# Retention values finished and evicted block by block, and a new order of VectorE's work in the input layer

## The chip, the cores and the metric

The kernel runs on one core of a Trainium2 chip. The time is the device time of one execution in microseconds (us), the median of several runs. The core has five engines that run side by side, each with its own queue of instructions: TensorE (PE in the profile, its weight loads PEld), VectorE (DVE), ScalarE (ACT), GpSimd (POOL) and SyncE (SP), which here only issues the loads from memory (HBM). They wait for one another by semaphores.

## What is computed

Two blocks of a language model in float32, for 512 tokens of width 1024. The change lies in the input layer of the first block:

```
n = _rms_norm(h, attn_norm_w[l])
proj = jnp.einsum('bsd,dc->bsc', n, w_in[l])
(gq, gk, gv, gg, ga, gb, rq, rk, rv, rg) = jnp.split(proj, split_idx, axis=-1)
o_gdn = _gated_deltanet(gq, gk, gv, gg, ga, gb, ...)
o_ret = _retention(rq, rk, rv, rg)
```

`rv` are the values of the retention, four heads of 128 columns. `rq` and `rk` are its queries and keys, which are rotated (`_xpos_rotary`) before use. The gated delta net needs, for each of 4 blocks of 128 tokens and each of 4 heads (16 tiles of 128x128), a matrix M and the inverse of I + M, and a masked product of queries and keys:

```
decay = jnp.exp(jnp.where(causal, diff, -jnp.inf))
m = jnp.where(strict, jnp.einsum('nbhik,nbhjk->nbhij', kb, kc) * decay, 0.0)
t_mat = lax.linalg.triangular_solve(eye + m, jnp.broadcast_to(eye, m.shape), ...)
qk = jnp.einsum('nbhik,nbhjk->nbhij', qc, kc) * decay
```

## The kernel before

**Projections.** Every projection is a matmul of 512 tokens by weights. A *unit* `u` is 128 output columns over the whole contraction of 1024, and is made of two *halves*, 2u and 2u+1, each over 512 of the contraction. float32 is split in a high and a low part, so that each product is three matmuls (lines 1930 to 1932, the helper `three`): a half is 12 matmuls of 128x512, a unit 24. The output lies in one of PSUM's banks 0 to 3, unit u in bank u mod 4; banks 4 to 7 (`MX`) are for the small matmuls of the delta net and the retention. Unit u may start when the bank of unit u-4 has been emptied: TensorE waits for `bank_free`, a counter that rises by one with each eviction.

**Weights.** They arrive by *pair* of units (p = u // 2), 1 MB in two transfers of 512 KB, into a buffer `raw` of two slots. ScalarE rounds a half to its high part (`split_hi(n)`, line 660, output `w_hi`), GpSimd makes the low part (`split_lo(n)`, line 539, output `w_lo`). Both buffers are rings of four halves: `split_hi(n)` waits until half n-4 has been used up (`half_done`, n-3), and until its pair has landed. SyncE issues pair p when the low parts of pair p-2 are made. So pair 10 (units 20 and 21, halves 40 to 43) is issued when `w_lo` of half 35 is there, and pair 11 when that of half 39 is.

**Units 12 to 15** are the retention's values, computed as one *wide* matmul: the 512 tokens are four blocks of 128 rows (one bank each), the 512 value columns are the moving side. Halves 24 to 31 are here the eight 128-rows of the contraction, k = 0 to 7. `wide_half(n)` runs one k over all four blocks, so all four banks are complete only at the end of k = 7. VectorE then empties them with a scale per token, `RCOL` (line 1514, output `ret_v`).

**Units 16 to 23** are the queries and keys of the retention. VectorE empties each by two instructions, `rotate_first` (lines 1299 and 1300: a product with the cosine, output `rq` or `rk`, and a shuffle of partitions, output `scratch`, which frees the bank), and finishes it by `rotate_second` (lines 1306 and 1307).

**The delta net beside them.** ScalarE takes the exponentials of two decay arrays, `T` and `M`, 128x2048 each (lines 832 and 834, semaphore `decay_exp`). VectorE makes M of its one by two products (lines 1471 and 1472, `m_ready`), and masks T (line 1480, by `UPPER`, called `masks` in the profile). T's last column goes to `KDC` (line 1483, output `small`) and T times the query-key product in banks 4 to 7 to `QKT` (line 1485, `qkt_ready`). For the inverses of the 8x8 blocks on M's diagonal, ScalarE cuts four pieces of M (line 839, `blocks_cut`) and writes the identity (line 841), VectorE reduces them (`cut_blocks`, lines 1354 to 1358) and eliminates (`eliminate(k)` for k = 1 to 6, lines 1363, 1366 and 1368). Line 1487 spreads the result over T (`t2_ready`). Between the two halves of unit 21 TensorE transposes T's 16 tiles (`t_transposes`, line 2154), and after unit 21 the levels of the inverse begin.

**What sets the order.** Everything is written out by hand: each engine's program is a loop over u, with `if u == ...` for the work beside the projections. An engine runs its instructions strictly in that order. GpSimd has one wait of its own: it starts the low parts of half 34 only after `m_ready` (before them, in its program, stand halves 32 and 33). In VectorE's program stand at u = 14 the two products of M, at u = 15 the four evictions of the values, and at u = 16 `rotate_first(16)`, the inverses, the mask on T, `KDC`, `QKT`, line 1487, and then `rotate_second(16)`, the rotations of 17, 18 and 19.

Of the kernel before, what the change touches and what calls it, by code (L numbers as in the profile page):

```python
# [9 lines left out]
P = 128  # L10
S = 512
D = 1024
KT = D // P
NB = S // P
H = 4
# [18 lines left out]
ACT = mybir.ActivationFunctionType  # L34
# [34 lines left out]
BK = 8  # L69
# [59 lines left out]
def build(nc, a, const, out):  # L129
    ctx = ExitStack()  # L130
    with ctx:
# [5 lines left out]
        def sem(name):  # L137
            return ctx.enter_context(nc.semaphore(name))
# [184 lines left out]
        qd_ready = sem("qd_ready")  # L323
        so_filled, o_ready, s_ready = sem("so_filled"), sem("gdn_o_ready"), sem("state_ready")
        gate_done, head_gated = sem("gate_silu"), sem("head_gated")
        ff_conv, ff_silu = sem("ff_conv"), sem("ff_silu")
        sc_filled, sc_ready, p_exp, p_ready = (sem("scores_filled"), sem("scores_max"),
                                               sem("probs_exp"), sem("probs_ready"))
# [303 lines left out]
        def _(act):  # L632
# [34 lines left out]
            def split_first(u):  # L667
                if u not in QUADS and u - 1 not in QUADS and u not in (U1 + 2, U1 + 3, U2 + 2):
                    split_hi(2 * u + 3)
# [112 lines left out]
            def ret_out(h):  # L782
                act.wait_ge(ro_filled, h + 1)
                nc.scalar.activation(RV[:, h, :, :].rearrange("p b i -> p (b i)"), PS[:, 6, :], ACT.Copy) \
                    .then_inc(ro_ready, 1)

            def ret_norm(r):
                table(LN_EXP_SET)
                act.wait_ge(rssq_filled, r + 1)
                rr = RR[:, 2 * r:2 * r + 2, :]  # L790
                step(nc.scalar.activation(rr, MX[:, 0:2, :], ACT.Ln, bias=CB[:, 0:1], scale=1.0 / P))
                nc.scalar.activation(rr, rr, ACT.Exp, scale=-0.5).then_inc(rr_ready, 1)
# [5 lines left out]
            for u in range(U1, U2):  # L798
                if u == 14:
                    split_hi(32)  # L800
                else:
                    split_first(u)
                    if u == 26:
                        new_values(0)
                    split_second(u)
# [15 lines left out]
                if u == 13:  # L821
# [10 lines left out]
                    nc.scalar.activation(T[:, :, :], T[:, :, :], ACT.Exp).then_inc(dexp, 1)  # L832
                    act.wait_ge(dmm_ready, 2)
                    nc.scalar.activation(M[:, :, :], M[:, :, :], ACT.Exp, scale=-1.0).then_inc(dexp, 1)
                if u == 16:
                    act.wait_ge(c2_in, 80)
                    act.wait_ge(m_ready, 1)
                    for r in range(0, P, 32):
                        nc.scalar.activation(DQ[r:r + 32, :, :], M[r:r + 32, :, r:r + 32], ACT.Copy) \
                            .then_inc(blocks_cut, 1)  # L840
                    nc.scalar.activation(XD[:, :, :], EYEB.unsqueeze(1).broadcast_to([P, 16, BK]), ACT.Copy) \
                        .then_inc(blocks_cut, 1)
                if u in LEVEL_AT and u > T_AT:
                    inverse_columns(LEVEL_AT[u])
                if u in RET_GAP:
# [368 lines left out]
        def _(dve):  # L1214
            v = nc.vector
# [9 lines left out]
            def tile_done(u):  # L1225

                dve.wait_ge(half_done, halves_when_done(u))
# [123 lines left out]
            def cut_blocks():  # L1351

                dve.wait_ge(blocks_cut, 4)
                step(v.tensor_tensor(DQ[:, :, :], DQ[:, :, :], BLOCK32.unsqueeze(1).broadcast_to([P, 16, 32]), MUL))
                step(v.tensor_tensor(DH[:, :, :], DQ[:, :, 0:16], DQ[:, :, 16:32], ADD))
                step(v.tensor_tensor(DB[:, :, :], DH[:, :, 0:8], DH[:, :, 8:16], ADD))
                dve.wait_ge(blocks_cut, 5)
                step(v.tensor_tensor(XD[:, :, 0:1], XD[:, :, 0:1], DB[:, :, 0:1], SUB))

            def eliminate(k):  # L1360

                w = k + 1
                step(v.stream_shuffle(XS[:, :, :].rearrange("p a c -> p (a c)"),
                                      XD[:, :, :].rearrange("p a c -> p (a c)"),
                                      [i // BK * BK + k for i in range(32)]))
                step(v.tensor_tensor(XP[:, :, 0:w], XS[:, :, 0:w],
                                     DB[:, :, k:k + 1].broadcast_to([P, 16, w]), MUL))
                step(v.tensor_tensor(XD[:, :, 0:w], XD[:, :, 0:w], XP[:, :, 0:w], SUB))
# [51 lines left out]
            for u in range(U1, U2):  # L1420
# [31 lines left out]
                if u == 13:  # L1452
# [13 lines left out]
                    v.tensor_scalar(T[:, :, :], TT[:, :, :], 0.0, None, ALU.min).then_inc(dmm_ready, 1)  # L1466
                    v.tensor_scalar(M[:, :, :], TT[:, :, :], 0.0, None, ALU.max).then_inc(dmm_ready, 1)
                if u == 14:
                    dve.wait_ge(lb_ready, 1)
                    dve.wait_ge(dexp, 2)  # L1470
                    step(v.tensor_tensor(M[:, :, :], M[:, :, :], LB[:, :, :], MUL))
                    v.tensor_tensor(M[:, :, :], GRAM[:, :, :], M[:, :, :], MUL).then_inc(m_ready, 1)
                if u == 16:
                    dve.wait_ge(m_ready, 1)
                    tile_done(16)
                    rotate_first(16)
                    cut_blocks()
                    for k in range(1, BK - 1):
                        eliminate(k)
                    v.tensor_tensor(T[:, :, :], T[:, :, :], UPPER.unsqueeze(1).broadcast_to([P, 16, P]), MUL) \  # L1480
                        .then_inc(dt_ready, 1)
                    dve.wait_ge(dt_ready, 1)
                    v.tensor_copy(KDC.unsqueeze(2), T[:, :, P - 1:P])
                    dve.wait_ge(qk_filled, 1)
                    v.tensor_tensor(QKT[:, :, :], MX16, T[:, :, :], MUL).then_inc(qkt_ready, 1)
                    dve.wait_ge(qkt_ready, 1)
                    v.tensor_tensor(T[:, :, :].rearrange("p a (b c) -> p a b c", c=BK),
                                    XD[:, :, :].unsqueeze(2).broadcast_to([P, 16, P // BK, BK]),
                                    by_block(BLOCK), MUL).then_inc(t2_ready, 1)
# [10 lines left out]
                        operand_lo(8 + h, RV[:, h, :, :].rearrange("p b i -> p (b i)"), XA[:, h, 1, :],  # L1500
                                   XA[:, h, 0, :])

                if not 12 <= u < 15 and not 17 <= u < 24:
                    tile_done(u)
                if u == 0:
                    dve.wait_ge(rstd_ready, 1)
                if u < 12:
                    conv_tile(u)
                elif u < 15:
                    pass  # L1510
                elif u == 15:
                    dve.wait_ge(rcol_ready, 1)
                    for b in range(NB):
                        v.tensor_scalar(RV[:, :, b, :], PS[:, b, :].rearrange("p (h d) -> p h d", h=H),
                                        RCOL[:, b:b + 1], None, MUL).then_inc(bank_free, 1)
                elif u < 24:
                    for n in ROTATED_AT.get(u, ()):
                        tile_done(n)
                        if n > 16:
                            rotate_first(n)  # L1520
                        rotate_second(n)
                else:
                    v.tensor_tensor(GT[:, u - 24, :], PS[:, u % 4, :], RSTD[:, :], MUL).then_inc(bank_free, 1)
# [396 lines left out]
        def _(pe):  # L1920
# [121 lines left out]
            def wide_half(n, X, fill=None, last_of=None):  # L2042
# [15 lines left out]
                        ins.then_inc(last_of, 1)  # L2058
                ins.then_inc(half_done, 1)

            def last_blocks(n0):

                for b in range(NB):
                    for k in range(4, KT):
                        n = n0 + k
                        if b == 0:
                            pe.wait_ge(w_hi, n + 1)
                            pe.wait_ge(w_lo, n + 1)
                        w, wl = (r[:, n % 4, :, :].rearrange("p t c -> p (t c)") for r in (WH, WL))
                        xh, xl = (XB[:, k, q, b * P:(b + 1) * P] for q in range(2))  # L2070
                        ins = three(PS[:, (M8 + 4 + b) % 4, :], xh, xl, w, wl, False, k == KT - 1)
                        if b == NB - 1:
                            ins.then_inc(half_done, 1)
                        elif k == KT - 1:
                            ins.then_inc(y_done, 1)
# [180 lines left out]
                ins.then_inc(rssq_filled, 1)  # L2256

            for u in range(U1, U2):
                if 12 <= u < 16:
                    wide_half(2 * u, XA)  # L2260
                    wide_half(2 * u + 1, XA)
                elif u == T_AT:
                    unit(u, u, XA, between=t_transposes)
                elif u == 26:
                    unit(u, u, XA, between=lambda: new_values(0))
                elif u == 31:
                    unit(u, u, XA, between=lambda: key_state(3), third=lambda: new_values(3))
                else:
                    unit(u, u, XA, fill=0 if u == 0 else None, midway=0)
# [329 lines left out]
```

## Time and profile before

| | us |
|---|---|
| median of 3 runs (1103.13 to 1104.79) | 1103.23 |
| span of the profiled execution | 1103.1 |
| TensorE busy | 1083.9 (98%) |
| VectorE busy | 671.5 (61%) |
| GpSimd busy | 499.8 (45%) |
| ScalarE busy | 456.3 (41%) |

The span goes from the first to the last instruction of the profiled execution, and is within 0.2 us of the median; no other time of that execution is given. "Busy" adds up an engine's instructions, however long each took; a matmul that runs at half the clock counts as busy for twice the time. The clock granted to TensorE stands in a column of its own (1.00 is full speed). All times "at" which something happens are counted from the start of the span.

### The profile page before, as it was taken

What the parts mean: (1) busy time and instruction counts of PE and PEld (TensorE: products, weight loads), DVE (VectorE), ACT (ScalarE), POOL (GpSimd) and SP (SyncE); (2) the same over time, 40 slices, a digit from 0 to 9 for tenths busy, and PEclk for the clock granted to TensorE, in tenths of its full rate; (3) what the DMA queues carried; (4) which work ended last, traced back from release to release, by engine and by line L of the source; (5) the groups of instructions that cost most, each with busy time, mean ns of one, the idle gap of its engine ahead of it and who ended that gap; (6) DMA issues with size and microseconds to landing.
All of it is one profiled execution on the core that took longest, in us unless ns stands there. A gap on an engine that the chain in (4) does not pass through costs nothing.

```text
span 1103.1 us, 16146 instructions
## 1 busy us (share of the span) xinstructions
PE 1083.9 (98%) x5882; PEld 876.1 (79%) x5882; DVE 671.5 (61%) x971; ACT 456.3 (41%) x801; POOL 499.8 (45%) x375
## 2 busy tenths in 40 slices
PE   8999989999999999999999999999999999999997
PEld 7788768788788888888888888877778778888786
DVE  6876776516766666666641222548754757986863
ACT  6335312255744333333333334345464543243663
POOL 5444632132455444444444445433347686632451
PEclk9999989999999999999999999999999999999999
DMA  9954612151223323232322325322115222212222
GB/s 245 136 86 72 81 40 40 37 134 59 77 89 102 114 76 114 76 114 76 114 73 99 105 79 151 115 77 78 39 51 141 54 80 78 77 40 78 77 77 77
DMA packets 101722, 97.29 MB, mean 88 GB/s; under 512 B 4896, under 2 KB 95776, under 8 KB 101280
## 3 DMA queue, kind: packets, MB, share of 16 engines
q1 hardware_dynamic: 101232, 95.71, 31.9%
q8 instruction: 39, 0.64, 0.2%
q10 hardware_dynamic: 432, 0.79, 0.2%
q14 instruction: 19, 0.16, 0.0%
HBM read 94.38 MB, written 2.10 MB: 87 GB/s over the span
## 4 chain that ended last, share of the span: by engine, by line
PE 88%; DVE 7%; ACT 2%; issue 2%; DMA 0%; POOL 0%; POOLq 0%; DVEq 0%; SPq 0%; ACTq 0%
PE ps L1930 25%; PE ps L1932 25%; PE ps L1931 25%; PE ps L2467 4%; DVE x_a L1232 1%; PE ps L2134 1%; DVE acc L1243 1%; DVE conv L1774 1%; PE ps L2402 1%; PE ps L2413 1%; DVE tt L1344 1%; ACT x_a L677 1%; PE ps L2390 1%; PE ps L2184 1%; PE ps L2169 0%
## 5 line engine op out<-in xcount | busy, mean ns | idle before, releaser
L539 POOL TENSOR_TENSOR w_lo<-raw,w_hi 128x512 fp32r<-128x512 f32 (+1 forms) x330 | 446.9, 1364 | 573.6 <-ACT w_hi L660 573.2
L660 ACT ACTIVATE w_hi<-raw 128x512 fp32r<-128x512 f32 (+1 forms) x330 | 201.4, 621 | 260.7 <-PE ps L1932 249.4
L1930 PE MATMUL ps<-x_a,w_hi 128*128 128x512 f32 x624 | 253.3, 406 | 10.2 <-DVE scratch L1300 3.5
L1932 PE MATMUL ps<-x_a,w_lo 128*128 128x512 f32 x624 | 245.0, 393 | 0.0
L1931 PE MATMUL ps<-x_a,w_hi 128*128 128x512 f32 x624 | 244.7, 392 | 0.0
L1930 PE MATMUL ps<-x_b,w_hi 128*128 128x512 f32 x416 | 162.5, 391 | 0.1
L1932 PE MATMUL ps<-x_b,w_lo 128*128 128x512 f32 x416 | 161.9, 389 | 0.0
L1931 PE MATMUL ps<-x_b,w_hi 128*128 128x512 f32 x416 | 161.9, 389 | 0.0
L1930 PEld LDWEIGHTS ps<-x_a,w_hi 128*128 128x128 f32 x624 | 118.1, 189 | 44.7 <-issue 9.1
L1931 PEld LDWEIGHTS ps<-x_a,w_hi 128*128 128x128 f32 x624 | 118.3, 190 | 25.1 <-issue 2.2
L1932 PEld LDWEIGHTS ps<-x_a,w_lo 128*128 128x128 f32 x624 | 118.0, 189 | 25.4
L1930 PEld LDWEIGHTS ps<-x_b,w_hi 128*128 128x128 f32 x416 | 78.1, 188 | 17.5 <-issue 0.8
L1931 PEld LDWEIGHTS ps<-x_b,w_hi 128*128 128x128 f32 x416 | 78.1, 188 | 16.4 <-issue 0.2
L1932 PEld LDWEIGHTS ps<-x_b,w_lo 128*128 128x128 f32 x416 | 78.1, 188 | 16.1
L1774 DVE TENSOR_TENSOR conv<-ps,conv 32x511 f32<-32x511 f32 (+2 forms) x96 | 65.5, 682 | 17.2 <-ACT conv L1106 14.4
L1930 PE MATMUL ps<-mlp_act,w_hi 128*128 128x512 f32 x176 | 68.5, 389 | 0.0
L1931 PE MATMUL ps<-mlp_act,w_hi 128*128 128x512 f32 x176 | 68.5, 389 | 0.0
L1932 PE MATMUL ps<-mlp_act,w_lo 128*128 128x512 f32 x176 | 68.5, 389 | 0.0
L1584 DVE TENSOR_TENSOR ps<-ps,rstd 128x512 f32<-128x512 f32 x44 | 30.7, 698 | 58.3 <-PE ps L1932 53.6
L1609 DVE TENSOR_TENSOR res<-ps,res 128x512 f32<-128x512 f32 x8 | 5.5, 686 | 83.0 <-PE ps L1932 83.0
L941 ACT ACTIVATE mlp_act<-prod_f 128x512 f32 (+1 forms) x22 | 13.9, 632 | 81.2 <-DVE prod_f L1596 81.2
L2467 PE MATMUL ps<-glu_hi,tap_w 32*128 32x512 f32 x512 | 43.2, 395 | 0.0
(349 smaller groups left out, 1502.5 us busy)
## 6 DMA issues: line engine op xcount, KB each, us to landing
raw<-in_w_up SPq DMA_DIRECT2D x44, 512.0 KB, 4.0
raw<-in_w_in SPq DMA_DIRECT2D x31, 512.0 KB, 8.0
raw<-in_c_w_in SPq DMA_DIRECT2D x24, 512.0 KB, 4.6
raw<-in_a_w_in SPq DMA_DIRECT2D x18, 512.0 KB, 4.5
raw<-in_w_down SPq DMA_DIRECT2D x16, 512.0 KB, 3.9
raw<-in_w_out SPq DMA_DIRECT2D x8, 512.0 KB, 4.0
raw<-in_c_w_out SPq DMA_DIRECT2D x8, 512.0 KB, 4.2
raw<-in_w_down SPq DMA_DIRECT2D x8, 384.0 KB, 3.3
```

The costliest lines, as they stand in the source:

```text
L539: nc.gpsimd.tensor_tensor(ring_half(WL, n), raw_half(n), f32(ring_half(WH, n)), SUB) \
L660: nc.scalar.activation(ring_half(WH, n), raw_half(n), ACT.Copy).then_inc(w_hi, 1)
L677: nc.scalar.activation(dst, src, ACT.Copy, scale=scale).then_inc(op_hi, 1)
L941: nc.scalar.activation(ACTS[:, bass.ds(n + (j - 2), 1), 0, :] .rearrange("p a s -> p (a s)"), PRODF[:, j - 2, :], ACT.Copy) \
L1232: v.scalar_tensor_tensor(out=dst_lo, in0=src, scalar=scale, in1=f32(dst_hi), op0=MUL, op1=SUB) \
L1243: v.tensor_tensor(ACC[:, :], ACC[:, :], sq, ADD).then_inc(acc_done, 1)
L1584: v.tensor_tensor(x, PS[:, j, :], RSTD[:, :], MUL).then_inc(bank_free, 1)
L1774: ins = v.tensor_tensor(y, PS[32 * q:32 * q + 32, 4 + r, 0:S - late_by], y, ADD)
L1930: mm(out, w_hi_, x_hi_, start=first, stop=False)
L1931: mm(out, w_hi_, x_lo_, start=False, stop=False)
L1932: return mm(out, w_lo_, x_hi_, start=False, stop=last)
L2467: ins = mm(PS[:, 4 + r, :], w, g[p, k % 2, TAP_PHASES * j:TAP_PHASES * j + S], start=first, stop=last)
```

## The change

It has three parts.

1. TensorE: halves 30 and 31 (k = 6 and 7 of the wide matmul) are no longer run k by k over the four blocks but block by block, both k for block 0, then for block 1, and so on (`ret_value_blocks`). After each of the first three blocks `ret_v_block_done` rises; after the last, `half_done` has risen twice. The matmuls are the same 24.
2. ScalarE: it evicts the four blocks with the scale per token, each when it is done, between `split_hi(33)` and `split_hi(34)`. The cutting of M's diagonal (`copy_blocks`) now stands ahead of `split_hi(36)` and no longer behind it.
3. VectorE: the evictions leave it. The mask on T goes ahead of M's two products and waits for the first exponential alone. `KDC` and `QKT` go ahead of the inverses, and `rotate_first(16)` goes behind `cut_blocks`.

```
+            def ret_values():
+                act.wait_ge(rcol_ready, 1)
+                act.wait_ge(bank_free, 12)
+                for b in range(NB):
+                    if b < NB - 1:
+                        act.wait_ge(rv_done, b + 1)
+                    else:
+                        act.wait_ge(half_done, halves_when_done(15))
+                    nc.scalar.activation(RV[:, :, b, :], PS[:, b, :].rearrange("p (h d) -> p h d", h=H),
+                                         ACT.Copy, scale=RCOL[:, b:b + 1]).then_inc(bank_free, 1)
...
+                    if u == 15:
+                        split_first(u)
+                        ret_values()
+                    else:
+                        split_first(u)
+                    if u == 16:
+                        copy_blocks()
...
                 if u == 14:
+                    dve.wait_ge(dexp, 1)
+                    v.tensor_tensor(T[:, :, :], T[:, :, :], UPPER.unsqueeze(1).broadcast_to([P, 16, P]), MUL) \
+                        .then_inc(dt_ready, 1)
                     dve.wait_ge(lb_ready, 1)
                     dve.wait_ge(dexp, 2)
...
                 if u == 16:
                     dve.wait_ge(m_ready, 1)
-                    tile_done(16)
-                    rotate_first(16)
-                    cut_blocks()
-                    for k in range(1, BK - 1):
-                        eliminate(k)
-                    v.tensor_tensor(T[:, :, :], T[:, :, :], UPPER.unsqueeze(1).broadcast_to([P, 16, P]), MUL) \
-                        .then_inc(dt_ready, 1)
                     dve.wait_ge(dt_ready, 1)
                     v.tensor_copy(KDC.unsqueeze(2), T[:, :, P - 1:P])
                     dve.wait_ge(qk_filled, 1)
                     v.tensor_tensor(QKT[:, :, :], MX16, T[:, :, :], MUL).then_inc(qkt_ready, 1)
+                    cut_blocks()
+                    tile_done(16)
+                    rotate_first(16)
+                    for k in range(1, BK - 1):
+                        eliminate(k)
...
-                elif u == 15:
-                    dve.wait_ge(rcol_ready, 1)
-                    for b in range(NB):
-                        v.tensor_scalar(RV[:, :, b, :], PS[:, b, :].rearrange("p (h d) -> p h d", h=H),
-                                        RCOL[:, b:b + 1], None, MUL).then_inc(bank_free, 1)
...
+            def ret_value_blocks():
+                for b in range(NB):
+                    for k in (6, 7):
+                        n = 24 + k
+                        if b == 0:
+                            pe.wait_ge(w_hi, n + 1)
+                            pe.wait_ge(w_lo, n + 1)
...
+                        ins = three(PS[:, b, :], xh, xl, w, wl, False, k == KT - 1)
+                        if b == NB - 1:
+                            ins.then_inc(half_done, 1)
+                        elif k == KT - 1:
+                            ins.then_inc(rv_done, 1)
```

VectorE's queue from the clamped decay arrays on, before the change (a row is engine instruction, output <- inputs by the program's names, shape, and the semaphores it waits for; `ps` is PSUM, `masks` the constant masks, `ret_v` the retention's values):

```order
L1467 TENSOR_SCALAR m<-tt 128x2048
L1471 TENSOR_TENSOR m<-m,lb 128x2048 [waits decay_exp,lb_ready]
L1472 TENSOR_TENSOR m<-k_gram,m 128x2048 [waits dve_step]
L1514 TENSOR_SCALAR ret_v<-ps,rstd_col 128x4x128 [waits rcol_ready,half_done]
L1514 TENSOR_SCALAR ret_v<-ps,rstd_col 128x4x128 x3
L1299 TENSOR_TENSOR rq<-ps,cos_sin 128x512 [waits half_done,m_ready]
L1300 STREAM_SHUFFLE scratch<-ps 128x512 [waits dve_step]
L1354 TENSOR_TENSOR blocks_cut<-blocks_cut,masks 128x512 [waits blocks_cut]
```

and the same place with the change (`t<-t,masks` is the mask on T, `small<-t` is `KDC`, `qkt` the masked query-key product):

```order
L1488 TENSOR_SCALAR m<-tt 128x2048
L1491 TENSOR_TENSOR t<-t,masks 128x2048 [waits decay_exp]
L1495 TENSOR_TENSOR m<-m,lb 128x2048 [waits decay_exp,lb_ready]
L1496 TENSOR_TENSOR m<-k_gram,m 128x2048 [waits dve_step]
L1500 COPY small<-t 128x16 [waits dt_ready,m_ready]
L1502 TENSOR_TENSOR qkt<-ps,t 128x2048 [waits qk_filled]
L1375 TENSOR_TENSOR blocks_cut<-blocks_cut,masks 128x512 [waits blocks_cut]
L1376 TENSOR_TENSOR blocks_half<-blocks_cut 128x256 [waits dve_step]
L1377 TENSOR_TENSOR blocks<-blocks_half 128x128 [waits dve_step]
L1379 TENSOR_TENSOR blocks_inv<-blocks_inv,blocks 128x16 [waits blocks_cut,dve_step]
L1320 TENSOR_TENSOR rq<-ps,cos_sin 128x512 [waits half_done,dve_step]
L1321 STREAM_SHUFFLE scratch<-ps 128x512 [waits dve_step]
```

The four evictions are gone, the mask, `KDC` and `QKT` have moved ahead, and the first rotation stands behind the cutting of the blocks.

ScalarE's queue from the two exponentials on, before the change (each `w_hi` is one `split_hi`, the first of them half 32):

```order
L832 ACTIVATE t<-t 128x2048 [waits dmm_ready]
L834 ACTIVATE m<-m 128x2048 [waits dmm_ready]
L660 ACTIVATE w_hi<-raw 128x512 [waits half_done,raw_in0] x4
L660 ACTIVATE w_hi<-raw 128x512 [waits half_done,raw_in1]
L839 ACTIVATE blocks_cut<-m 32x512 [waits m_ready,const2_in]
L839 ACTIVATE blocks_cut<-m 32x512 x3
L841 ACTIVATE blocks_inv<-masks 128x128
L660 ACTIVATE w_hi<-raw 128x512 [waits half_done,raw_in1] x3
```

and with the change:

```order
L861 ACTIVATE t<-t 128x2048 [waits dmm_ready]
L863 ACTIVATE m<-m 128x2048 [waits dmm_ready]
L661 ACTIVATE w_hi<-raw 128x512 [waits half_done,raw_in0] x2
L797 ACTIVATE ret_v<-ps,rstd_col 128x4x128 [waits ret_v_block_done,bank_free,rcol_ready]
L797 ACTIVATE ret_v<-ps,rstd_col 128x4x128 [waits ret_v_block_done] x2
L797 ACTIVATE ret_v<-ps,rstd_col 128x4x128 [waits half_done]
L661 ACTIVATE w_hi<-raw 128x512 [waits half_done,raw_in0] x2
L805 ACTIVATE blocks_cut<-m 32x512 [waits m_ready,const2_in]
L805 ACTIVATE blocks_cut<-m 32x512 x3
L807 ACTIVATE blocks_inv<-masks 128x128
L661 ACTIVATE w_hi<-raw 128x512 [waits half_done,raw_in1] x4
```

Between halves 33 and 34 now stand the four evictions, and half 36 has gone behind the cut of the blocks. The queues of GpSimd and SyncE hold the same instructions in the same order.

## Rows read from the trace of the kernel before

**Rows 1.** The page: the chain that ended last, by engine.
```profile
PE 88%; DVE 7%; ACT 2%; issue 2%; DMA 0%; POOL 0%; POOLq 0%; DVEq 0%; SPq 0%; ACTq 0%
```

**Rows 2.** TensorE in order: start us, us, instruction, idle before it and releaser.
```profile
112.90 0.39 PE L1932 MATMUL ps<-w_hi,x_a 128*128 128x512 f32 x1
115.37 0.50 PE L1930 MATMUL ps<-x_a,w_hi 128*128 128x512 f32 x1 [2.08 <-DVE ret_v L1514]
...
122.59 0.39 PE L1930 MATMUL ps<-x_a,w_hi 128*128 128x512 f32 x1
...
144.12 0.39 PE L1932 MATMUL ps<-x_a,w_lo 128*128 128x512 f32 x1
148.02 0.80 PE L1930 MATMUL ps<-x_a,w_hi 128*128 128x512 f32 x1 [3.51 <-DVE scratch L1300]
...
155.41 0.48 PE L1930 MATMUL ps<-x_a,w_hi 128*128 128x512 f32 x1
...
172.79 1.91 PE L2169 MATMUL ps<-ident,tt 128*128 128x128 f32 x16
```

**Rows 3.** Stretches: length, PE busy (instructions), granted clock, DMA share, GB/s.
```profile
115.30:122.60 7.30, 7.23 (x25) 0.77 0.42 40
122.60:128.10 5.50, 5.50 (x26) 1.00 0.96 85
148.00:155.40 7.40, 7.38 (x28) 0.58 0.02 7
```

**Rows 4.** VectorE in order of time, 109 to 148 us.
```profile
109.07 2.29 DVE L1471 TENSOR_TENSOR m<-m,lb 128x2048 f32<-128x2048 f32 x1 [2.72 <-ACT m L834]
111.39 3.26 DVE L1472 TENSOR_TENSOR m<-k_gram,m 128x2048 f32<-128x2048 f32 x1
114.58 2.71 DVE L1514 TENSOR_SCALAR ret_v<-ps,rstd_col 128x512 f32<-128x512 f32 x4
122.86 0.69 DVE L1299 TENSOR_TENSOR rq<-ps,cos_sin 128x512 f32<-128x512 f32 x1 [5.57 <-PE ps L1932]
...
136.20 2.29 DVE L1480 TENSOR_TENSOR t<-t,masks 128x2048 f32<-128x2048 f32 x1
138.53 1.15 DVE L1483 COPY small<-t 128x16 f32<-128x16 f32 x1
139.59 2.28 DVE L1485 TENSOR_TENSOR qkt<-ps,t 128x2048 f32<-128x2048 f32 x1
...
147.25 0.72 DVE L1300 STREAM_SHUFFLE scratch<-ps 128x512 f32<-128x512 f32 x1
```

**Rows 5.** ScalarE: first exponential, the cut of M, the high part of half 40.
```profile
105.25 1.92 ACT L832 ACTIVATE t<-t 128x2048 f32<-128x2048 f32 x1 [4.02 <-DVE t L1466]
...
120.44 2.58 ACT L839 ACTIVATE blocks_cut<-m 32x512 f32<-32x512 f32 x4
...
132.03 0.63 ACT L660 ACTIVATE w_hi<-raw 128x512 fp32r<-128x512 f32 x1 [3.11 <-DMA raw<-in_w_in]
```

**Rows 6.** ScalarE's nearest evictions from PSUM: a whole bank; scaled, in four pieces.
```profile
216.03 0.60 ACT L784 ACTIVATE ret_v<-ps 128x512 f32<-128x512 f32 x1 [8.44 <-PE ps L2134]
216.90 1.15 ACT L751 ACTIVATE vb<-ps,small 128x128 f32<-128x128 f32 x4 [0.28 <-PE ps L2208]
```

**Rows 7.** GpSimd: low parts of half 32, of halves 33 and 34, of half 43.
```profile
109.56 2.94 POOL L539 TENSOR_TENSOR w_lo<-raw,w_hi 128x512 fp32r<-128x512 f32 x1 [5.43 <-ACT w_hi L660]
112.47 4.57 POOL L539 TENSOR_TENSOR w_lo<-raw,w_hi 128x512 fp32r<-128x512 f32 x2
...
139.88 1.30 POOL L539 TENSOR_TENSOR w_lo<-raw,w_hi 128x512 fp32r<-128x512 f32 x1 [0.24 <-ACT w_hi L660]
```

**Rows 8.** Pair 10's loads: issue ns, when issued, landing; landing of pair 4's.
```profile
L379 SPq DMA_DIRECT2D raw<-in_w_in x2: 368/438/508, 118.3 to 118.7; - x2
DMA to landing us min/median/max: 8.4/10.9/13.3
...
DMA to landing us min/median/max: 5.8/8.1/10.4
```

More of the change, by code:

```diff
@@ L325, in build @@
         gate_done, head_gated = sem("gate_silu"), sem("head_gated")
+        rv_done = sem("ret_v_block_done")
         ff_conv, ff_silu = sem("ff_conv"), sem("ff_silu")
@@ L785, in ret_out, with copy_blocks @@
                     .then_inc(ro_ready, 1)
+            def ret_values():
[8 more added lines that the diff above has]
+                                         ACT.Copy, scale=RCOL[:, b:b + 1]).then_inc(bank_free, 1)
+            def copy_blocks():
+                act.wait_ge(c2_in, 80)
+                act.wait_ge(m_ready, 1)
+                for r in range(0, P, 32):
+                    nc.scalar.activation(DQ[r:r + 32, :, :], M[r:r + 32, :, r:r + 32], ACT.Copy) \
+                        .then_inc(blocks_cut, 1)
+                nc.scalar.activation(XD[:, :, :], EYEB.unsqueeze(1).broadcast_to([P, 16, BK]), ACT.Copy) \
+                    .then_inc(blocks_cut, 1)
             def ret_norm(r):
@@ L801, in _ @@
                 else:
-                    split_first(u)
+                    if u == 15:
[5 more added lines that the diff above has]
+                        copy_blocks()
                     if u == 26:
@@ L834, in _ @@
                     nc.scalar.activation(M[:, :, :], M[:, :, :], ACT.Exp, scale=-1.0).then_inc(dexp, 1)
[L835 to L842, printed above, removed]
                 if u in LEVEL_AT and u > T_AT:
@@ L1501, in _ @@
                                    XA[:, h, 0, :])
-                if not 12 <= u < 15 and not 17 <= u < 24:
+                if not 12 <= u < 16 and not 17 <= u < 24:
                     tile_done(u)
@@ L1508, in _ @@
                     conv_tile(u)
-                elif u < 15:
+                elif u < 16:
                     pass
-                elif u == 15:
-                    dve.wait_ge(rcol_ready, 1)
-                    for b in range(NB):
-                        v.tensor_scalar(RV[:, :, b, :], PS[:, b, :].rearrange("p (h d) -> p h d", h=H),
-                                        RCOL[:, b:b + 1], None, MUL).then_inc(bank_free, 1)
                 elif u < 24:
@@ L2059, in wide_half @@
                 ins.then_inc(half_done, 1)
+            def ret_value_blocks():
[5 more added lines that the diff above has]
+                            pe.wait_ge(w_lo, n + 1)
+                        w, wl = (r[:, n % 4, :, :].rearrange("p t c -> p (t c)") for r in (WH, WL))
+                        xh, xl = (XA[:, k, q, b * P:(b + 1) * P] for q in range(2))
+                        ins = three(PS[:, b, :], xh, xl, w, wl, False, k == KT - 1)
[3 more added lines that the diff above has]
+                            ins.then_inc(rv_done, 1)
             def last_blocks(n0):
@@ L2258, in _ @@
             for u in range(U1, U2):
-                if 12 <= u < 16:
+                if 12 <= u < 15:
                     wide_half(2 * u, XA)
                     wide_half(2 * u + 1, XA)
+                elif u == 15:
+                    ret_value_blocks()
                 elif u == T_AT:
```

## The prediction

> **What bounds the kernel now.** I read the chain that ended last first: TensorE is 88% of it [rows 1]. So the change can only gain or lose where TensorE stands still or runs slowly, and the next view is TensorE in order of time through units 15 to 21 [rows 2]. There are two stops. The last matmul of unit 15 starts at 112.90 us and unit 16 only at 115.37: 2.08 us idle, released by VectorE's first eviction of the values. And unit 21 starts at 148.02, 3.51 us idle, released by the shuffle of `rotate_first(17)`. The stretches show a second loss: after the first stop the granted clock is 0.77 on average over 115.3 to 122.6, after the second 0.58 over 148.0 to 155.4, between them 1.00 [rows 3]. At the lower of its two levels, 1.2 GHz, a matmul takes twice as long; it fell behind both stops, when TensorE had stood idle 2 and 3.5 us.
>
> **What both stops cost.** At full clock, units 17 to 20 go from 122.59 to 144.12, 95 starts apart: 0.227 us a matmul, 5.44 a unit, 2.72 a half [rows 2].
> First stop: without it unit 16 would start at 112.90 + 0.23 = 113.13 and unit 17 at 118.57; it starts at 122.59. Cost 4.02 (2.24 late start, 1.78 slow clock).
> Second: unit 21 is due at 144.12 + 0.23 = 144.35. Its first half takes 2.72, the 16 transposes 1.91 at full clock (the same sixteen at 172.79), so its second half is due at 148.98; it starts at 155.41. Cost 6.43 (3.67 late start, 2.76 slow clock) [rows 2].
> Together 10.45. That is the ceiling; the rest asks what the change leaves of it.
>
> **Part 1, TensorE and ScalarE's evictions.** The last two halves of the values are the same 24 matmuls, 5.44 us, ending at 113.1. Run by block, block 0 is complete 6 matmuls after their start at about 107.7, at 109.1, then one block every 1.36 us. ScalarE comes free for it after its second exponential (105.25 + 1.92 + about 1.9 = 109.0) and two high parts of about 0.6 each, at 110.1. The trace has no such scaled eviction of a bank into four heads. Its bounds are a whole bank in 0.60 and a scaled one in four pieces, 1.15 [rows 6]; I take 0.65, since it is one instruction. Block 0 is out at 110.8 (111.3 at the upper bound), unit 16 needs its bank at 113.13: no wait in either case. Block 3 is out at 114.0, unit 19 needs it at 129.5. High parts 34 and 35 now stand behind the evictions and are made at 114.6 and 115.2; unit 17 needs the low ones at 118.6 and 121.3. VectorE loses 2.71 us of evictions [rows 4] and no longer stands at them when M is made at 114.65. The first stop goes: 4.02.
>
> **Part 2, VectorE's order.** T's mask (2.29, [rows 4]) moves from 136.20 into VectorE's idle 2.72 us ahead of M: the first exponential ends at 107.17 [rows 5], so the mask runs from 107.2 to 109.5 and M's first product starts at 109.5, not 109.07. `KDC` and `QKT` (1.15 and 2.28) fill part of the 5.57 us in which VectorE waited for unit 16 [rows 4]. Followed through: M is done at 115.3, `KDC` and `QKT` at about 118.8; the four cuts of M, which `cut_blocks` waits for, are there at 115.3 + 2.58 = 117.9 [rows 5]. `rotate_first(16)`, `cut_blocks` and the six eliminations took 122.86 to 136.20, 13.3 us with all the turns that they waited for GpSimd; that leads to 132.1. From the start of line 1487 (139.59 + 2.28 = 141.9) to the end of the shuffle of 17 (147.97) it is 6.1 more: 138.2 at the latest, since small instructions that met GpSimd less often would save some us. Unit 21 wants its bank at 113.13 + 5 x 5.44 = 140.3: 2 us of room. Line 1487 is done by 134.5, the transposes want it at 143. The second stop goes as well: 6.43.
>
> **What is late next: the weights.** Low part of half 32: 2.94 us beside M's products, that of half 43 beside `QKT`, which reads PSUM: 1.30. And M's second product, beside it, takes 3.26 where the mask takes 2.29 [rows 4, 7]. The ends fit turns: product to 111.4, half 32 to 112.5, second product to 114.65, half 33 to about 115.8. With the change the first product ends at 111.8, half 32 at 113.0 (needed 113.13), the second product at 115.3, half 33 at 116.5; TensorE wants it at 113.13 + 2.72 = 115.85. That is a new wait of 0.65. If instead GpSimd gets in ahead of the first product, half 33 is there at 114.4 and M comes at 116.7: no wait at 33, and half 34 is made by 118.0, in time. The Trainium skill, page SBUF — State Buffer, section Who interferes with whom, says that a VectorE instruction with two SBUF inputs and a GpSimd one that reads SBUF shut each other out for a whole instruction, and that the order of issue decides who waits. By that rule, where the mask pushes the first product onto the very start of half 32's low part, the sum is either of those two; the trace agrees with the turns (2.94 against 1.30). I take the first, 0.65.
> Halves 34 and 35 follow to 119.1 (before 118.3), when pair 10 is issued. Its second transfer lands 13.3 us after an issue at 118.7 [rows 8], and high part 40 starts at 132.03 [rows 5]; with the change at about 132.8. Its low part is there at 132.8 + 0.6 + 1.3 = 134.7, or 135.5 if it waits its turn. Unit 20 wants it at 113.13 + 0.65 + 4 x 5.44 = 135.5. Before, it was wanted at 138.9, and the 3.11 us that ScalarE waited for this load cost nothing; that cover shrinks to under 1 us. I take 0.2.
> Sum: 4.02 + 6.43 - 0.65 - 0.2 = 9.6. The profiled execution's span is 1103.1, the median 1103.23, so the forecast is 1103.2 - 9.6 = 1093.6. From 155.41 on everything waits for what is shifted with it, and I expect no change there.
>
> **The rivals.**
> A. *The load of pair 10 becomes the wait.* Pair 11 is issued when half 39's low part is made: half 35 is used up at 124.7, then come 0.6 and 1.3, so at about 126.5, while pair 10 is still landing until 132.8. If both share the engines equally, the 6.3 us that are left of pair 10 double: it lands at 139.1, TensorE waits until 141.0 instead of 135.5, and 2.8 of slow clock follow as after the 3.5 us stop. 9.6 + 0.2 - 5.5 - 2.8 leaves 1.5: 1101.7. If they only mix a little, 2 us are lost: 1095.6. For it: unit 20's margin is under 1 us, and while pair 10 lands the DMA share is 0.96 [rows 3]. Against: pair 4's second transfer landed in 10.4 us [rows 8] with a load of 1 MB issued right behind it, so a follower does not make a pair slow. The Trainium skill, page DMA: Bandwidth & Descriptors, section Two DMAs through the same engine are not ordered, says that descriptors of one queue start in order but are pipelined; by that pair 11 costs pair 10 little, and no run here shows it by itself.
> B. *The small wait drops the clock.* 0.65 us idle at half 33 brings the slow stretch that followed the first stop, 1.78: 1095.4. The trace has stops of 2.08 and 3.51 with a fall behind them; what 0.65 does it does not show.
> C. *Only the first stop goes.* If VectorE's shuffle of 17 is later than 140.3, for instance because turns with GpSimd lengthen each small instruction, part of 6.43 stays: with 2 us of stop and 1.8 of slow clock 1097.4. The 2 us of room speak against it.
> D. *Slower: the cut of M holds up the weights.* High part 36 now stands behind the four cuts, which wait for M. Low part 36 is there at M + 2.58 + 0.3 + 0.6 + 1.3 = M + 4.8, unit 18 wants it at 124.7; from M at 119.9 on each us of M is a us of TensorE, with 2.8 of slow clock behind it. The gain of 9.8 is used up when M comes at 127; at 128.5, for 1104.7. M is expected at 115.3 to 116.7 from rows, so ten unexplained us are wanted.
>
> **How the numbers follow.** Forecast (one small wait or none, 1092.8 to 1094.4): 0.72. A: mild 0.10, hard 0.03. B: 0.08. C: 0.04. D: 0.03. The lower end is the ceiling, 1103.2 - 10.45 = 1092.8, less 0.2 for the spread of runs, 1092.6; the upper end takes in mild A and B, 1096.5, and leaves hard A, C and D out, 0.1 together. A measurement tells 0.2% (2.2 us) from no change: faster means under 1101. All of the forecast, mild A, B and C are: 0.94. Hard A is within 0.2%: 0.03. Slower 0.03.
>
> **What would show it.** Right: no TensorE idle before the first matmul of units 16 and 21, clock 1.00 from 107 to 150, unit 21's second half starting near 145; four scaled evictions of 0.6 to 0.7 on ScalarE between 110 and 114; VectorE's mask at 107.2, its shuffle of 17 done by 138.2. A wait of under 1 us for a low part in the middle of unit 16, and pair 10's high part at 132.5 to 133. Wrong: TensorE idle for GpSimd's low part at unit 20 (A), a clock under 1.00 in unit 16 or 17 (B), a stop before unit 21 (C) or 18 (D).

## The result and the profile after

The changed kernel takes 1094.98 us (median of 4 runs, 1094.5 to 1095.14), the kernel before, beside it, 1103.99 (4 runs, 1103.13 to 1104.79): ratio 0.9935, 95% interval 0.9916 to 0.9953. In five more rounds it was 1094.67 (6 runs, 1094.56 to 1095.23) against 1101.51 (13 runs, 1099.57 to 1104.37): 0.9937 (0.9924 to 0.995). By both ratios the gain in device time is about 7 us. The medians lie 9.0 us apart the first time and 6.8 the second, so with this spread of the kernel before, 5 to 9 us is what can be said. Between the two first profiled executions it is 10.5 (1103.1 and 1092.6 us of span). That difference, and how far the kernel before spreads, is what the experiments had to explain.

First the page of the changed kernel, its busy times and its chain:

```profile
PE 1080.2 (99%) x5882; PEld 874.0 (80%) x5882; DVE 667.1 (61%) x967; ACT 458.7 (42%) x805; POOL 498.8 (46%) x375
...
PE 90%; DVE 5%; ACT 2%; issue 1%; POOL 1%; DMA 1%; POOLq 0%; DVEq 0%; SPq 0%; ACTq 0%
```

TensorE's share of the chain has risen from 88% [rows 1] to 90%. TensorE in order of time at the two places of the stops (columns as in [rows 2]; here lines 1947 to 1949 are the three matmuls, 2187 the transposes):

```profile
112.64 0.39 PE L1949 MATMUL ps<-w_hi,x_a 128*128 128x512 f32 x1
112.86 0.39 PE L1947 MATMUL ps<-x_a,w_hi 128*128 128x512 f32 x1
...
115.36 0.39 PE L1949 MATMUL ps<-x_a,w_lo 128*128 128x512 f32 x1
116.01 0.47 PE L1947 MATMUL ps<-x_a,w_hi 128*128 128x512 f32 x1 [0.26 <-POOL w_lo L540]
...
140.36 0.39 PE L1949 MATMUL ps<-x_a,w_lo 128*128 128x512 f32 x1
140.59 0.39 PE L1947 MATMUL ps<-x_a,w_hi 128*128 128x512 f32 x1
...
143.32 1.91 PE L2187 MATMUL ps<-ident,t 128*128 128x128 f32 x16
144.98 0.48 PE L1947 MATMUL ps<-x_a,w_hi 128*128 128x512 f32 x1
```

Unit 16 follows unit 15 without a gap, and so does unit 21 unit 20 (140.36 to 140.59 is one step of 0.23). What is left is a step of 0.65 instead of 0.23 at 115.36, in the middle of unit 16, where GpSimd's low part of half 33 is waited for: 0.42 us. (The trace calls 0.26 of it idle, since a matmul is still counted as busy after the next one could have started; the step behind it, 0.31, adds 0.08.) The clock in stretches that answer to [rows 3] is 1.00 throughout:

```profile
112.80:118.70 5.90, 5.64 (x25) 1.00 0.00 1
118.70:124.10 5.40, 5.40 (x26) 1.00 0.77 75
...
140.50:145.50 5.00, 5.00 (x32) 1.00 0.93 183
```

VectorE, against [rows 4], and ScalarE's evictions, which no row of before showed, each in order of time:

```profile
106.92 2.29 DVE L1491 TENSOR_TENSOR t<-t,masks 128x2048 f32<-128x2048 f32 x1 [0.84 <-ACT t L861]
109.13 2.29 DVE L1495 TENSOR_TENSOR m<-m,lb 128x2048 f32<-128x2048 f32 x1
111.45 3.27 DVE L1496 TENSOR_TENSOR m<-k_gram,m 128x2048 f32<-128x2048 f32 x1
...
133.95 0.73 DVE L1321 STREAM_SHUFFLE scratch<-ps 128x512 f32<-128x512 f32 x1
```

```profile
109.64 1.39 ACT L797 ACTIVATE ret_v<-ps,rstd_col 128x512 f32<-128x512 f32 x2
111.70 0.69 ACT L797 ACTIVATE ret_v<-ps,rstd_col 128x512 f32<-128x512 f32 x1 [0.67 <-PE ps L1949]
113.06 0.69 ACT L797 ACTIVATE ret_v<-ps,rstd_col 128x512 f32<-128x512 f32 x1 [0.67 <-PE ps L1949]
```

The mask has slipped into VectorE's wait; the idle of 2.72 us ahead of M's products is 0.84 ahead of the mask. The shuffle of unit 17 is done at 134.7 and not at 148.0. A scaled eviction costs ScalarE 0.69, and the last two wait for their block to be complete.

### The profile page after: what moved, and what is told of

The parts are those of the page before. It is cut to its first block, busy times and chain, and to the rows that moved or that the text cites. A ratio compares the mean times of both kernels' runs of the same rounds, so it can differ in the third digit from the quotient of the medians.

```text
span 1092.6 us, 16148 instructions
## 1 busy us (share of the span) xinstructions
PE 1080.2 (99%) x5882; PEld 874.0 (80%) x5882; DVE 667.1 (61%) x967; ACT 458.7 (42%) x805; POOL 498.8 (46%) x375
## 4 chain that ended last, share of the span: by engine, by line
PE 90%; DVE 5%; ACT 2%; issue 1%; POOL 1%; DMA 1%; POOLq 0%; DVEq 0%; SPq 0%; ACTq 0%
PE ps L1947 26%; PE ps L1949 25%; PE ps L1948 25%; PE ps L2502 4%; DVE x_a L1253 1%; PE ps L2167 1%; POOL w_lo L540 1%; DVE acc L1264 1%; DVE conv L1791 1%; PE ps L2437 1%; PE ps L2448 1%; DVE tt L1365 1%; PE ps L2425 1%; PE ps L2217 1%; ACT x_a L678 1%
```

## The experiments

For comparing traces I use one stretch: from the start of VectorE's clamping of T (`t<-tt`, at 102.9 to 103.6) to the first of unit 21's transposes. From the first transpose to the end it took 949.2 to 949.9 us in every trace, so the stretch holds nearly the whole effect; what is left outside is the slow transposes, 0.4 us, in the profiles where the clock is still low there.

| kernel | stretch, us | stops in it, us idle | slow clock in it, us | span |
|---|---|---|---|---|
| before, first profile | 50.17 | 2.08, 3.51 | 3.8 | 1103.1 |
| full change | 40.45 | 0.26 | 0 | 1092.6 |
| full change again (a0) | 40.46 | 0.27 | 0 | 1092.7 |
| blocks and ScalarE only (e2) | 42.16 | 1.72 | 0 | 1094.9 |
| VectorE's order only (e3) | 44.23 | 2.41 | 1.6 | 1096.6 |
| ScalarE at the end (e4) | 41.08 | 0.86 | 0 | 1093.5 |
| blocks only (e5) | 50.13 | 2.08, 3.52 | 3.8 | 1103.0 |
| splits early (e6) | 39.92 | none | 0 | 1092.3 |
| pair 10 from other columns (e7) | 40.45 | 0.27 | 0 | 1093.0 |
| mask late (e8) | 41.90 | 0.29, 0.91 | 0 | 1095.0 |
| before (b1) | 47.68 | 2.08, 2.66 | 2.2 | 1100.6 |
| before (b2) | 45.26 | 2.06, 2.66 | 0 | 1097.5 |
| before (b3) | 46.70 | 2.08, 2.66 | 1.2 | 1099.4 |
| before (b4) | 46.63 | 2.08, 2.66 | 1.0 | 1099.1 |

(Slow clock: the sum of what steps between the 128x512 matmuls took above 0.227, where they were near 0.43; rounded. It leaves out the first step behind a stop, single slower steps of some 0.1 us in each, and the slow transposes.)

**a0, the full change again.** No edit.

> The changed kernel once more, five rounds beside the kernel before. The traces of the two differ by 10.5 us of span (1103.1 against 1092.6), the first timed runs by a ratio of 0.9935 (0.9916 to 0.9953), which is 5 to 9 us. Theory: the whole 10.5 us of the trace are device time, and the first comparison fell short because of the spread of the kernel before: ratio 0.9905 to 0.992. Rival: the timed runs gain less than the profiled one, since something outside the span or a state that the profile does not show takes 2 to 3 us back: 0.993 to 0.9945 again.

Measured: 0.9937 (0.9924 to 0.995), inside the rival's numbers. The theory that the first comparison fell short by chance is out. But the other half of the rival, that the changed kernel gives something back, is not what was seen: its trace is the same again, 1092.7. It is the kernel before that is often faster than its first profile. Its 13 timed runs of these rounds, each with its span and mean granted clock, point to the clock: the eight with spans of up to 1100.2 had 0.998 to 1.000, the five from 1100.3 up to 1102.4 had 0.994 or 0.995.

**b1 to b4, the kernel before, profiled four more times.** No edit.

> The kernel before itself, looked at again (four looks in all, b1 to b4). Its timed runs spread over 5.2 us (1099.57 to 1104.79), those of the full change over 0.7 (1094.5 to 1095.23). Theory: the stops of 2.1 and 3.5 us are the same in every execution (they are the work of VectorE), but the clock does not fall equally long behind them; the 4.5 us of slow clock counted in the profiled execution are there in full only in the slowest, and each look's span is about 1098.5 plus its own slow clock behind the two stops. Rival: the clock falls alike every time and the stops differ in length from execution to execution; then the looks show the same slow clock and idle times that differ by up to 5 us.

> As b1: by the theory the idle times are 2.1 and 3.5 us again, the slow clock behind them between 0 and 4.5 us, and the span differs from 1103.1 by just that.

> As b1: by the theory idle 2.1 and 3.5 us, slow clock 0 to 4.5 us, span 1098.5 plus the slow clock.

> As b1: by the theory idle 2.1 and 3.5 us, slow clock 0 to 4.5 us, span 1098.5 plus the slow clock.

Measured: times 1102.47, 1099.43, 1101.35 and 1101.05, spans 1100.6, 1097.5, 1099.4 and 1099.1. TensorE at the second stop in b2 and in b1, in order of time:

```profile
145.34 0.50 PE L1930 MATMUL ps<-x_a,w_hi 128*128 128x512 f32 x1 [2.66 <-DVE scratch L1300]
145.68 0.39 PE L1931 MATMUL ps<-x_a,w_hi 128*128 128x512 f32 x1
145.91 0.40 PE L1932 MATMUL ps<-x_a,w_lo 128*128 128x512 f32 x1
```

```profile
145.42 0.80 PE L1930 MATMUL ps<-x_a,w_hi 128*128 128x512 f32 x1 [2.66 <-DVE scratch L1300]
146.01 0.63 PE L1931 MATMUL ps<-x_a,w_hi 128*128 128x512 f32 x1
146.43 0.63 PE L1932 MATMUL ps<-x_a,w_lo 128*128 128x512 f32 x1
```

The same instruction, the same 2.66 us of idle, and one execution goes on at full clock, the other at half. The granted clock behind both stops, over 115.10 to 122.40 and 145.30 to 151.50, of b2, b3 and b1:

```profile
115.10:122.40 7.30, 7.22 (x32) 1.00 0.41 38
145.30:151.50 6.20, 6.16 (x35) 1.00 0.48 93
```

```profile
115.10:122.40 7.30, 6.82 (x30) 1.00 0.33 32
145.30:151.50 6.20, 5.72 (x26) 0.72 0.52 106
```

```profile
115.10:122.40 7.30, 7.14 (x31) 1.00 0.37 38
145.30:151.50 6.20, 6.08 (x16) 0.50 0.54 101
```

In none of the four did the clock fall behind the first stop, as it had in the first profile (0.77, [rows 3]) and in e5. Behind the second it fell in three, for 1.0, 1.2 and 2.2 us. So the theory holds for the clock, and the stretches go by it: above b2 they are longer by 1.37 (b4), 1.44 (b3) and 2.42 (b1), of which 0.25 is the first step behind the stop, 0.59 instead of 0.34. The spans differ a little more, by what lies ahead of the stretch and, in b1, the slow transposes. The theory falls for the second stop, which I had expected to be 3.5 us in each: it is 2.66 where the first stop is not followed by a slow stretch. That stretch makes TensorE 1.8 us later at unit 21 (due at 144.35 and not at 142.53, as in b2), but VectorE's shuffle of 17 2.7 us later (147.97 and not 145.29), so that slow clock behind one stop also lengthens the next. The chip is not what differs: on the one that ran b1 to b4 the kernel before took from 1099.43 to 1104.94 us. What makes the clock fall behind the same stop in one execution and not in the next stays open. The first profile had the slow clock behind both stops. And in b1 to b4 the time is 1.87 to 1.95 above the span, so that its own time must have been near 1105, at the top of the runs and not at their median. That is worked out; the time of that execution was not given.

**e2, blocks and ScalarE's evictions alone.** VectorE keeps the old order, without the evictions:

```
-  u == 14: wait dexp 1; T * UPPER
-  u == 16: KDC; QKT; cut_blocks(); tile_done(16); rotate_first(16); eliminate(1..6)
+  u == 16: tile_done(16); rotate_first(16); cut_blocks(); eliminate(1..6); T * UPPER; KDC; QKT
```

> TensorE's block order and ScalarE's evictions alone; VectorE has lost the evictions but keeps the old order (rotation of 16, inverses, mask on T, KDC, QKT, line for t2, rotation of 17). Theory: the two stops are separate. The first goes (4.0 us). VectorE starts on unit 16 when it is done, at 118.6 instead of 122.9, so everything behind comes 4.2 us earlier and the second stop before unit 21 stays whole, 3.5 us of idle and 2.8 us of slow clock: 4.0 us faster than before, 6.2 us slower than the full change, span about 1099. Rival: the stops are one, since the second comes from VectorE being late after the first: without the first stop VectorE catches up and the second shrinks to under 1 us, span about 1094.

Measured: 1096.81 (6 runs, 1096.54 to 1097.98), ratio 0.9956 (0.9942 to 0.9969). The span, 1094.9, is nearer to the rival's 1094 than to the theory's 1099, but the mechanism lies between the two: the first stop is gone and the second has shrunk to 1.72, neither 3.5 nor under 1:

```profile
142.74 0.50 PE L1946 MATMUL ps<-x_a,w_hi 128*128 128x512 f32 x1 [1.72 <-DVE scratch L1321]
```

The clock stayed at 1.00 behind it. Against b2, the execution of before without slow clock, the part is worth 45.26 - 42.16 = 3.1 us, and the order on top of it 42.16 - 40.45 = 1.7. So the stops are neither separate nor one: each part takes something from the second.

**e3, VectorE's order alone.** The same lines of VectorE moved as in the full change, in the kernel before; TensorE and ScalarE as before.

> VectorE's new order alone; the values are evicted by VectorE as before, after M. Theory: the first stop stays and grows by the 0.3 to 0.5 us by which the mask on T delays M, with its slow clock; the second goes: 6.4 - 0.4 = 6.0 us faster than before, span about 1097. VectorE's shuffle of unit 17 has then over 2 us of room. Rival (the mask is not free): M comes 2.3 us later, the first stop grows to 4.3 us and the gain is only 4 us, span 1099.

Measured: 1097.93 (8 runs, 1096.83 to 1099.72), ratio 0.9964 (0.995 to 0.9978). The first stop is 2.41 (before 2.08), the second is gone: the size of the delay by the mask, 0.33, is as the theory has it, and the stop did not grow to the rival's 4.3. The 6.0 us do not hold: they were reckoned from the first profile, and by the medians the gain is 1101.51 - 1097.93 = 3.6. The clock fell behind the stop here (the three matmul lines are one number higher in this kernel):

```profile
115.47 0.50 PE L1931 MATMUL ps<-x_a,w_hi 128*128 128x512 f32 x1 [2.41 <-DVE ret_v L1515]
```

```profile
115.40:122.60 7.20, 7.13 (x24) 0.76 0.41 36
```

A stop that is left also leaves a spread: 2.9 us over 8 runs here, 1.4 in e2, 0.7 in the full change. The fastest run here is 1.8 us below the profiled one (1098.6), about the price of this slow stretch; that its clock did not fall was not profiled.

**e4, ScalarE evicts, TensorE k by k.**

```
-                if 12 <= u < 15: ...
-                elif u == 15:
-                    ret_value_blocks()
+                if 12 <= u < 16:
+                    wide_half(2 * u, XA)
+                    wide_half(2 * u + 1, XA)
```

> The full change, but TensorE runs the last two halves of the values k by k as before, and ScalarE evicts the four blocks after their end. Theory: ScalarE starts at about 112.9 and has block 0 out at 113.6, so unit 16 starts 0.75 us late, and the low part of half 33 is no longer waited for beyond that; idle 0.6 to 0.8 us, no fall of the clock, span 0.4 to 0.5 us above the full change: the block order is worth half a microsecond, moving the evictions to ScalarE nearly everything. Rival: an idle of 0.7 us right before unit 16 lowers the clock as the stop of 2.08 us did, span 2 to 2.5 us above the full change.

Measured: one run, 1095.41; stretch 41.08, 0.63 above the full change, clock 1.00. The theory holds, with 0.1 us more of each than expected:

```profile
113.93 0.50 PE L1944 MATMUL ps<-x_a,w_hi 128*128 128x512 f32 x1 [0.86 <-ACT ret_v L794]
```

The block order is worth 0.6 us; VectorE's queue, not the time at which the banks are complete, made the first stop.

**e5, blocks alone.** `ret_value_blocks` in the kernel before, with VectorE waiting per block, in its old place and order.

> The block order alone: VectorE evicts block by block, in its old place behind M, and in its old order. Theory: the blocks are ready from 109 on, but VectorE is busy with M to 114.65, so nothing changes: both stops as before (2.1 and 3.5 us idle), span 1103. Rival: VectorE frees the banks for units 17 to 19 and the rotation earlier, which shortens the second stop: span 1100 to 1102.

Measured: one run, 1104.92, span 1103.0. The clock fell behind both stops here, as in the first profile of before, so that the two can be compared: stops of 2.08 and 3.52, stretch 50.13 against 50.17. The block order alone does nothing, as the theory says.

**e6, high parts 32 and 33 ahead of the exponentials.**

```
                     split_hi(31)
+                    split_hi(32)
+                    split_hi(33)
                     act.wait_ge(dmm_ready, 1)
```

> The full change, and the high parts of halves 32 and 33 are made ahead of ScalarE's two exponentials, where ScalarE waits 4.0 us for VectorE, and no longer behind them. GpSimd can then make their low parts before VectorE's products of M begin. Theory (turns between VectorE and GpSimd): low part 33 comes by about 105.5 and not 115.9, M's second product takes 2.3 us and not 3.27, the small wait in the middle of unit 16 (0.4 us) goes, span about 1092.2. Rival: the first exponential comes later, because a high part stands in its way when the clamped array is there, and the delay goes on to the mask and M; no gain, span 1092.6 or more.

Measured: 1094.18 (6 runs, 1093.95 to 1094.47), against 1094.56 to 1095.23 for the full change in the same rounds, no overlap; ratio to before 0.9931 (0.9918 to 0.9944). GpSimd made four low parts from 101.50 on, and TensorE's wait in unit 16 is gone:

```profile
101.50 6.99 POOL L540 TENSOR_TENSOR w_lo<-raw,w_hi 128x512 fp32r<-128x512 f32 x4
```

M's second product takes 2.29. The rival has a part in it: the four low parts last to 108.5 (105.5 was expected) and now meet the mask, which takes 3.37, so that M is made at 115.2 and not 114.7; TensorE does not wait for that. It is the fastest version that was run.

**e7, pair 10 from pair 11's columns.** `R + 256` becomes `R + 768` in the list of first columns, so that units 20 and 21 get the weights of units 22 and 23.

> The full change, but pair 10 is loaded from the columns of pair 11 (the rotated queries and keys of two heads are then wrong; this asks only about the load). In the full change pair 10's second transfer lands 13.4 us after its issue, pair 11's after 9.3. Theory (place in memory): it is the columns, the pair now lands in 7 to 9 us, ScalarE's high part of half 40 starts by 127.5 and no longer at 132.2; TensorE gains nothing, span within 0.2 us of the full change. Rival (moment): what else runs at 118 to 132 us slows it, it lands in 13 us again.

Measured: one run, 1094.9, span 1093.0, stretch 40.45. The load, in the view of `raw` (issue times; landing, us after the issue):

```profile
L380 SPq DMA_DIRECT2D raw<-in_w_in x2: 368/438/508, 118.8 to 119.2; - x2
...
DMA to landing us min/median/max: 7.0/8.0/9.0
```

It is the columns: 9.0 instead of 13.4 at nearly the same moment, and pair 11's own loads from these columns landed in 8.2 (before) and 9.3 (full change). What about them is slow was not tried. High part 40 started at 128.19, later than the 127.5 expected. TensorE gained nothing, so the load is not the bound. What the earlier weights did change is VectorE: GpSimd now makes low parts 40 to 42 beside its instructions, three of them take 0.90, 1.78 and 1.66 instead of 0.27, 0.68 and 0.69, and the shuffle of 17 is done at 137.8 and not at 134.7. TensorE takes that bank at 141.0.

**e8, the mask late.** `T * UPPER` moves from ahead of M's products to behind them.

> The full change, but the mask on T stays behind M (at the head of the work for unit 16), so that VectorE makes M 0.3 us earlier and everything behind the mask comes up to 2.3 us later. Theory (VectorE has room ahead of unit 21, 5.5 us in the full change's trace, and M's date only matters through GpSimd's turns): the low part of half 33 comes about 0.1 to 0.4 us earlier or at the same time, no stop before unit 21, span 1092.3 to 1092.8: the move of the mask is worth nothing by itself. Rival: with the mask late, KDC and QKT and the inverses come so late that the rotation of unit 17 is past 140.3 us and a stop before unit 21 returns, span 1094 or more.

Measured: one run, 1096.9, span 1095.0, 0.7 of which lies ahead of the stretch; the stretch is 41.90, 1.45 above the full change. My theory falls. The rival has the size of the span but not the reason: the shuffle of 17 is done at 137.3, in time. What is waited for is the low part of half 34, at the start of unit 17, and above all that of half 40, at the start of unit 20:

```profile
119.68 0.47 PE L1946 MATMUL ps<-x_a,w_hi 128*128 128x512 f32 x1 [0.29 <-POOL w_lo L540]
137.19 0.47 PE L1946 MATMUL ps<-x_a,w_hi 128*128 128x512 f32 x1 [0.91 <-POOL w_lo L540]
```

In this place the mask, which reads SBUF twice, runs while GpSimd makes low part 34. Both lose by it: the mask takes 3.27 instead of 2.29, the low part 3.33, where low part 34 of the full change, beside `KDC` and `QKT`, took 1.29:

```profile
115.11 3.27 DVE L1496 TENSOR_TENSOR t<-t,masks 128x2048 f32<-128x2048 f32 x1
```

```profile
112.89 6.64 POOL L540 TENSOR_TENSOR w_lo<-raw,w_hi 128x512 fp32r<-128x512 f32 x2
116.20 3.33 POOL L540 TENSOR_TENSOR w_lo<-raw,w_hi 128x512 fp32r<-128x512 f32 x1
```

(The first row is halves 33 and 34 together, the second is 34 by itself. Half 33 met M's second product, as it does in the full change.) So pair 10 is issued 2.4 us later, at 120.8 (1.7 when the 0.7 ahead of the stretch is taken off), its second transfer lands 13.5 after its issue, and ScalarE's high part 40 starts at 134.77 and not 132.20. This ends like the prediction's rival A in its mild form, TensorE waiting for low part 40, but pair 11 has no part in it: pair 10 is issued late.

## Where the prediction was right, and where it failed

1093.6 was forecast, 1094.98 measured, inside the range of 1092.6 to 1096.5. Both stops go as it says; its largest term was mis-sized, and that the number came out so near is in part luck, since errors met.

- *The first stop goes, 4.02.* It goes in each of the profiles. Its 2.24 us of late start are real in every profile of before; its 1.78 of slow clock are not: four of six profiles with this stop of 2.1 us have none.
- *The second stop goes, 6.43.* It goes; 3.67 of late start are 2.8 to 2.9 where the clock had not fallen before it (b1 to b4), and 2.76 of slow clock are 0 to 2.6 there.
- So the failed step is "Together 10.45. That is the ceiling": it took the slow clock of one execution, 4.5 us (1.78 and 2.76), as a standing cost. In b1 to b4 it was nothing behind the first stop and 0 to 2.6 behind the second. Without slow clock the same two stops are worth 45.26 - 40.45 = 4.8 us (b2), with all of it 9.7 within the stretch; the medians lie between, at 6.8 and 9.0.
- Against the one profile that it was read from, the sum is too small and not too large. The 16 transposes were put at 1.91, how long they are busy; from their start to the next matmul it is 1.66 (143.32 to 144.98), so that the second stop cost 6.68 there. With that, with 0.50 for the small wait (0.42 and the step of 0.31 behind it) and nothing for pair 10, it is 4.02 + 6.68 - 0.50 = 10.2, and the stretch with the transposes shrank by 9.72 + 0.44 = 10.2.
- *"The profiled execution's span is 1103.1, the median 1103.23, so the forecast is 1103.2 - 9.6".* The time is 1.9 above the span. That gives near 1105 for the profiled execution, and 1105.0 - 9.6 would have been 1095.4; taking the sum from the median instead made the forecast 1.8 too low, and the sum, 0.9 smaller than the 10.5 between the two spans, brought half of that back. That the two errors had opposite signs is luck.
- *ScalarE's evictions, 0.65, no wait for them.* 0.69. Right.
- *The new wait at half 33, 0.65.* 0.42, in the place and by the engine named. The first product ended at 111.42, not 111.8. M's first product started at 109.13 and GpSimd's half 32 at 109.29, and that half took 3.27 us instead of 1.3. By the Trainium skill's rule (SBUF — State Buffer, Who interferes with whom) the engine that issues first goes first; the trace agrees.
- *Pair 10, 0.2.* No wait; high part 40 at 132.20 (132.8 forecast), with pair 11 issued at 126.6 behind it, 3.7 us earlier than before (130.3). Landing was 13.4 against 13.3 [rows 8]: the follower cost pair 10 nothing; it took longer itself, 9.3 to its second landing against 8.2. So rival A is out as it was argued. The margin was as thin as said: in e8 TensorE waited as soon as low part 35 was done 2.4 us later.
- *The shuffle of 17 by 138.2.* 134.7, since VectorE met GpSimd less often; e7, where they met more often, shows it at 137.8. Rivals B, C and D: the clock did not fall behind the small wait, no stop was left, M was made at 114.7.

## What to carry to other kernels

Look at a kernel's slow clock in more than one execution before it enters a sum: the idle time of a stop is the work of the program, the clock behind it is not the same each time. Read what lies around the span from a run that gives both. And where two engines take turns on SBUF, the place of an instruction matters through whom it meets: the same mask delayed M by 0.3 us from VectorE's idle time, and from behind M it made the stretch 1.4 us longer, mostly by way of a weight load that was issued late.

## What the runs showed of the hardware

- A stop of TensorE of 2.06 to 2.08 us was followed by a fall from 2.4 to 1.2 GHz in two profiles of six, one of 2.66 in three of four. Stops of 0.26 to 0.91 (six in five profiles) and of 1.72 (one) had none behind them; behind 2.41 (one profile) and 3.5 (two) it fell.
- VectorE's 128x2048 product of two SBUF inputs took 2.28 or 2.29 us, and 3.26 to 3.37 where it had to take turns with a low part of GpSimd first; a low part that had to let such a product go first took 2.9 to 3.3 us instead of 1.3.
- A load of two transfers of 512 KB (pair 10) landed in 13.3 to 13.5 us in 13 profiles of 14, and in 9.0 in the one where it read pair 11's columns (e7).
- Pair 11, issued on the same queue while pair 10 was under way, did not slow pair 10; it paid itself: its second transfer landed in 8.0 to 8.3 us when pair 10 was 10 us or more ahead, in 9.1 to 9.5 with pair 10 8.1 to 8.4 ahead, and in 10.8 with 6.7 (e8).
- The time of an execution lay 1.8 to 2.0 us above its span in every run that gives both.
